# Moving score tiles, value products and the last norm within the step plan of a two-branch attention block

## What is computed

```python
h = rms_norm(x, norm_g)
(qa, ka, va, za, qb, kb, vb, zb, ga, gb) = split(h @ w_in)
# branch A: 8 query heads on 2 key/value heads, window of 2 chunks of 64, partial rotary, sinks
ya = swa_sink_attention(rope(qa), rope(ka), va, sinks) * silu(za)
# branch B: 8 heads, own chunk and 8 chunks before it, learned relative bias
yb = chunked_relpos_attention(qb, kb, vb, rel_bias) * silu(zb)
merged = sigmoid(ga + bias0) * (ya @ w_br_a) + sigmoid(gb + bias1) * (yb @ w_br_b)
out = rms_norm(x + merged @ w_out, final_g)
```

## Time and profile before

| | us |
|---|---|
| median of 3 runs | 3277.61 |
| lowest and highest | 3277.61, 3279.2 |
| the profiled execution, its time | 3279.67 |
| its span in the trace | 3277.8 |
| PE busy | 3209.7 (98%) |
| DVE busy, ACT busy, POOL busy | 1350.5, 1391.4, 1471.0 |

### The profile page before, as it was taken

One profiled execution on the slowest core, in us unless ns is written; L12 is line 12 of the kernel. 1 busy time (PEld: TensorE's weight loads), 2 busy tenths in 40 slices (PEclk: granted clock), 3 DMA queues, 4 the chain that ended last, 5 costly groups with the idle time before them and its releaser, 6 DMA issues.

```text
span 3277.8 us, 48058 instructions
## 1 busy us (share of the span) xinstructions
PE 3209.7 (98%) x15992; PEld 2468.7 (75%) x15992; DVE 1350.5 (41%) x2936; ACT 1391.4 (42%) x2929; POOL 1471.0 (45%) x1217
## 2 busy tenths in 40 slices
PE   7999999999999999999999999999999999999998
PEld 5777877788777887778877788777887778877786
DVE  3552345523455234552345523455134551345512
ACT  4453444433444334453444434444344443435432
POOL 5344554345543445434554344543445434543344
PEclk9999999999999999999999999999999999999999
DMA  4232532224322343222532235322353223432223
GB/s 158 75 92 89 172 108 70 76 94 168 108 70 76 94 169 107 70 76 94 172 104 70 76 94 174 103 70 75 97 170 105 71 75 96 173 102 70 69 93 116
DMA packets 114552, 339.26 MB, mean 104 GB/s; under 512 B 17392, under 2 KB 33904, under 8 KB 112112
## 3 DMA queue, kind: packets, MB, share of 16 engines
q1 hardware_dynamic: 114288, 335.95, 31.9%
HBM read 316.23 MB, written 17.04 MB: 102 GB/s over the span
## 4 chain that ended last, share of the span: by engine, by line
PE 85%; issue 8%; DVE 5%; ACT 2%; POOL 0%; DMA 0%; DVEq 0%; ACTq 0%; SPq 0%; POOLq 0%
PE acc L980 14%; PE acc L982 14%; PE acc L981 14%; PE ps_pt L1044 6%; PE ps_o L1075 6%; PE sc L980 4%; PE sc L982 4%; PE sc L981 4%; PE sc L1024 3%; PE sc L921 2%; PE sc L923 2%; PE sc L922 2%; PE sc L1015 2%; DVE sc L1315 1%; DVE negm L1323 1%
## 5 line engine op out<-in xcount | busy, mean ns | idle before, releaser
L802 POOL TENSOR_TENSOR w_lo<-w_raw,w_hi 128x512 fp32r<-128x512 f32 x928 | 1212.6, 1313 | 1717.2 <-ACT w_hi L1119 1716.4
L980 PE MATMUL acc<-h_hi,w_hi 128*128 128x512 f32 x2432 | 1005.0, 413 | 0.0
L982 PE MATMUL acc<-h_hi,w_lo 128*128 128x512 f32 x2432 | 952.8, 392 | 0.0
L981 PE MATMUL acc<-h_lo,w_hi 128*128 128x512 f32 x2432 | 949.9, 391 | 0.0
L1119 ACT ACTIVATE w_hi<-w_raw 128x512 fp32r<-128x512 f32 x928 | 579.0, 625 | 434.2 <-DMA w_raw<-w 114.3
L980 PEld LDWEIGHTS acc<-h_hi,w_hi 128*128 128x128 f32 x2432 | 457.6, 188 | 129.4 <-issue 54.0
L982 PEld LDWEIGHTS acc<-h_hi,w_lo 128*128 128x128 f32 x2432 | 456.7, 188 | 100.8
L981 PEld LDWEIGHTS acc<-h_lo,w_hi 128*128 128x128 f32 x2432 | 459.2, 189 | 75.9
L1207 ACT ACTIVATE probs_b<-sc,negm 128x640 f32<-128x640 f32 x256 | 203.4, 795 | 346.4 <-DVE negm L1323 345.4
L1214 ACT ACTIVATE probs_t<-ps_pt 128x512 f32<-128x512 f32 (+1 forms) x272 | 154.7, 569 | 393.1 <-PE ps_pt L1044 393.1
L1350 DVE SCALAR_TENSOR_TENSOR z<-th,sc 128x512 f32<-128x512 f32 x64 | 43.9, 685 | 497.4 <-PE sc L982 497.4
(11 more groups left out here) (134 smaller groups left out, 3798.2 us busy)
## 6 DMA issues: line engine op xcount, KB each, us to landing
w_raw<-w SPq DMA_DIRECT2D x464, 512.0 KB, 3.6
rows<-x SPq DMA_DIRECT2D x36, 512.0 KB, 7.3
xt<-x_t SPq DMA_DIRECT2D x16, 1024.0 KB, 10.1
part<-den_rows SPq DMA_DIRECT2D x128, 128.0 KB, 3.8
out<-rows SPq DMA_DIRECT2D x32, 512.0 KB, 2.8
x_in<-x SPq DMA_DIRECT2D x28, 512.0 KB, 5.4
cs<-rope_tab SPq DMA_DIRECT2D x8, 512.0 KB, 3.6
den_rows<-rden_t SPq DMA_DIRECT2D x256, 1.0 KB
```

Of the source, the lines that this page charges most:

```text
L802: pool.tensor_tensor(w_lo[n % 2][:, c], w_raw[n % 2][:, c], w_hi[n % 2][:, c].bitcast(FP32), ALU.subtract).then_inc(w_split, 1)
L980: pe.matmul(dst[:, :], hi, src_hi[:, row, :], start=begin, stop=False)
L981: pe.matmul(dst[:, :], hi, src_lo[:, row, :], start=False, stop=False)
L982: mm = pe.matmul(dst[:, :], lo, src_hi[:, row, :], start=False, stop=end)
```

## The change

Four edits. In `A_BEATS`, S0 now stands ahead of V0 V1. In `B_BEATS`, S0 S1 stand ahead of V0 V1, and S2 S3 ahead of V2 V3. `FIRST_SCORES` puts pair 4's third and fourth score tiles one quarter later each, so that all four are three quarters apart. The last pair gets a string of its own, with `den_load` ahead of V2 V3 and `norm` after the seventh quarter where it was after the last.

```diff
-A_BEATS = "T0 F G T1 F H D T2 V0 V1 S0 F E0 T3 F F C S1 V2 V3 F E1 F S2 F E2 F L F S3 F E3 F N"
-B_BEATS = "F T0 F G T1 F H D T2 F T3 F C V0 V1 S0 S1 T4 F E0 T5 F E1 T6 F T7 F L V2 V3 S2 S3 T8 F E2 T9 F T10 E3 F N V4 V5 V6"
+A_BEATS = "T0 F G T1 F H D T2 S0 V0 V1 F E0 T3 F F C S1 V2 V3 F E1 F S2 F E2 F L F S3 F E3 F N"
+B_BEATS = "F T0 F G T1 F H D T2 F T3 F C S0 S1 V0 V1 T4 F E0 T5 F E1 T6 F T7 F L S2 S3 V2 V3 T8 F E2 T9 F T10 E3 F N V4 V5 V6"
+LAST_BEATS = "T0 F G T1 F H D T2 V0 V1 F T3 F F C L V2 V3 F F N F F F F F"
-FIRST_SCORES = (9, 12, 14, 17)
+FIRST_SCORES = (9, 12, 15, 18)
-        for beat in (A_BEATS if s < PAIRS else B_BEATS).split():
+        for beat in (LAST_BEATS if nxt is None else A_BEATS if s < PAIRS else B_BEATS).split():
```

## The result

The changed kernel takes **3262.05 us** (median of 5 runs, 3258.16 to 3263.42) against 3278.57 before (5 runs, 3277.61 to 3279.9): a ratio of 0.9948 with a 95% interval of 0.9936 to 0.996, or 17 us less, between 13 and 21. The forecast was 3261.0 in 3253 to 3270.

A forecast was written before the change was run, and what follows sets the result against it. PE, busy 98% of the span, bounds the kernel, so only its some 27 us of stops can pay. Seven later blocks at 1.82 (12.7) plus the first block's 3.9 make 16.6 us off 3277.61: 3261.0, range 3253 to 3270.

The forecast's parts named there:

- First scores: Pair 4's score tiles: two stops of 2.07 us go, one of 1.04 comes; net 1.03 us per later block.
- the replay: Pair 4's step times recomputed from the old trace's starts with the third and fourth score tiles each one quarter later.
- the chain of 5.34 us: Path through DVE and ACT from one score tile's start to the next one's release, taken as 5.34 us.
- The first rival: Exponentials overlap `turned`, so no new wait before pair 4's first transposes: 7.3 us more gained, 3253.7; chance 0.10.
- the few other stops for exponentials: Said to be smaller ones at the third score tile of a B pair, left as they are by the change.
- Last pair: End of each block: with `norm` gone from between, `whole` and all behind it come 0.79 us earlier.
- The rival that the edit brings nothing: Last pair: `part` is late or something else holds `whole`; costs 6.3 us, giving 3267.3; chance 0.08.
- Scores ahead of values: The 88 reordered bursts: a step costs the same whatever follows, so the reordering is costed at 0.
- 7.9 us each way: Bound on the reordering: 88 bursts at 0.09 us per change of matmul shape; as slower rival 3268.9, chance 0.12.
- The slower rival: Issue work at value heads exposed behind score tiles, up to 0.30 us a burst, 26.2 us, 3287.2; chance 0.05.
- First block: Gains 3.9 us: 2.1 from first scores, 0.8 from the last pair, 1.0 from stops at value heads.
- The sum: Seven later blocks 12.7 us and first block 3.9, together 16.6 us less than before: 3261.0 us.

The follow-up runs named there:

- e1: Kernel before with only FIRST_SCORES changed to (9, 12, 15, 18): 3268.41 us, ratio 0.997 to the kernel before.
- e4: Changed kernel with the exponentials of pair 4's fourth score tile put ahead of `turned` (job v 0) on ACT: 3255.24 us, ratio 0.9926 to the kernel before.
- e5: Changed kernel with FIRST_SCORES = (9, 12, 15, 17), so only the third tile is later than before: 3263.49 us, ratio 0.9953 to the kernel before.
- e2: Kernel before with only the last pair's own string (LAST_BEATS) added: 3271.41 us, ratio 0.9978 to the kernel before.
- e6: Changed kernel with the last pair's `norm` put back to the end of its beats, `den_load` left early: 3267.19 us, ratio 0.9967 to the kernel before.
- e3: Kernel before with only the A_BEATS and B_BEATS edits, scores ahead of values: 3277.09 us, ratio 0.9996 to the kernel before.
- e7: Changed kernel with the first burst of every B pair as S0 V0 S1 V1 instead of S0 S1 V0 V1: 3271.6 us, ratio 0.9979 to the kernel before.
- e8: e4's kernel with B_OUT beginning (0, 1): ACT copies a B pair's first transposes, DVE the second: 3246.55 us, ratio 0.99 to the kernel before.
- e9: e8's kernel with the last pair's gate and gate_rest straight behind its norm, ahead of job gb 2 and job ya 0: 3241.62 us, ratio 0.9886 to the kernel before.

## Why the prediction was right

- **First scores.** Forecast: two stops of 2.07 us go, one of 1.04 comes, in seven blocks. The trace shows the stops gone, the new one in its place, and the start of the transposes within 0.01 us of the replay; e1 gives the edit's own time, e4 and e5 show that the new stop is `turned` ahead of the exponentials and that without it the chain of 5.34 us just suffices. The first rival, that the new stop wouldn't be there, was wrong, and e4 is what it would have been worth. One reading of the forecast was wrong without touching a term of its sum: the few other stops for exponentials are not smaller. They are three, all in the first block, of 1.46, 0.49 and 0.49 us, and the change leaves them as they are.
- **Last pair.** Forecast 0.79 us a block. e2 shows 0.74 by the starts in the fourth and 0.76 on average, and e6 that it is `norm`'s place. The rival that the edit brings nothing is refuted.
- **Scores ahead of values.** Forecast 0, with 7.9 us each way. e3 shows 0 within 0.04 us in the fourth block. Scores straight behind transposes and B's values behind A's scores, which no row showed, cost what the other entries do. The slower rival, exposed value heads, is refuted by the same run: the idle of PEld for issue reads 75.5 us in 269 stops against 73.4 in 246, yet a later block as a whole became no longer.
- **First block.** Forecast 3.9 us, of which the value heads' stops 1.0. These rows, before and after, hold it:

```profile
43.80 0.39 PE L980 MATMUL acc<-h_hi,w_hi 128*128 128x512 f32 x1
...
268.56 0.47 PE L980 MATMUL sc<-y_hi,w_hi 128*128 128x512 f32 x1 [1.01 <-DVE y_lo L1426]
```

```profile
41.96 0.39 PE L981 MATMUL acc<-h_hi,w_hi 128*128 128x512 f32 x1
...
262.31 0.47 PE L981 MATMUL sc<-y_hi,w_hi 128*128 128x512 f32 x1 [0.22 <-DVE y_lo L1427]
```

  From the first quarter of `k 4` to the second half of `br 0` it is 224.76 and 220.35: 4.4 us gained, 0.5 more than forecast. By the same measure e1 gains 2.2, e3 1.2 and e2 0.7. Followed along the quarters, the gain comes in three steps: 2.3 us by the end of pair 4's score tiles, where the forecast had taken 2.1 over from the fourth block; 1.3 at the four value heads, where it had the 1.0 of idle time; and 0.8 at the end, as forecast. At the first value head 0.32 us were gained for 0.27 shown: idle time leaves out the part of a stop that the modelled end before it covers.
- **The sum.** The seven later blocks gain 12.8 us in the trace and the first 4.4, together 17.2 inside the blocks, against 16.6 forecast and 17 measured. The mechanism and its sizes are shown; that the time came within 1.1 us of the 3261.0 is in part luck. The gain is measured to 4 us either way only, and the median from which the 16.6 was taken off, 3277.61 by three runs, is 3278.57 by five. The trace also has what no term covers: from the second half of `br 0` to the next block's start, where no step was moved, a block of the loop takes 136.6 to 138.8 us in these two executions. The eight such stretches, the last one to the end, sum to 1096.4 us before and 1097.9 after.

## What to carry to other kernels

Where one engine is at 98%, list its stops with their releasers and replay each from start to start; starts gave every step here to 0.01 us, while idle times shorten each stop by the modelled tail. When a producer is moved later, look for what it falls behind on its engine and how near its consumer has come: the second half of this gain was lost to one PSUM copy (`turned`) that now stood ahead of two exponentials, and putting them back in front of it was worth another 6.8 us. Move what waits, and leave the order within a burst alone unless it changes how often the matmul shape changes.

## What the runs showed of the hardware

Two more changes between matmuls on 64 rows and matmuls on 64 columns cost 0.35 us a burst in e7, where the whole burst is 3.07; that their order is free (e3) was expected only by bounds. The profiled executions also differ by 1.4 to 1.8 us in the first 44 us of the launch: tile `k 4` starts at 43.80 before and 41.96 after, with nothing changed ahead of it. e1, e3, e4, e5, e6 and e7 have the early start (41.96 to 42.22), e2, e8 and e9 the late one (43.59 to 43.80). The granted TensorE clock tells them apart. From 25.8 to 31.0 us the answers are, before and after (start and end, length, busy time of each engine, then the clock as a share of full speed):

```profile
25.80:31.00 5.20, 5.20 (x16) 4.12 (x17) 5.20 (x9) 0.59 (x2) 3.69 (x3) 0.67 0.42 114
```

```profile
25.80:31.00 5.20, 5.20 (x24) 4.28 (x24) 5.20 (x9) 0.63 (x1) 3.50 (x3) 1.00 0.42 117
```

It is 0.67 in the four late executions and 1.00 in the seven early ones. Before, it is 0.50 from 27.6 to 30.6, the lower of the clock's two levels (1.2 GHz), and matmuls there start 0.43 us apart where they start 0.23 apart after the change: eight matmuls, 1.6 us. Before that stretch PE had stood idle for `w_lo`, up to 25.73, for 1.79 us; after the change it had for 1.15, up to 25.51, and then ran on at 2.4 GHz. This stop is 1.79 to 2.35 us long in the four late executions and 0.80 to 1.75 in the seven early ones; that it sets off the drop is likely, but no run here tests it. Some 1.6 us is therefore a floor under what one profiled execution against another can tell.
